# Latent attention keys in pairs of heads, with the shared rotated rows prepared once a layer

## What is computed

```python
def mla_mixer(c_q, c_kv, k_rope, ...):
    q = (rms_norm(c_q, q_norm_g) @ w_uq).reshape(b, t, MLA_HEADS, MLA_QK)
    kv = (rms_norm(c_kv, kv_norm_g) @ w_ukv).reshape(b, t, MLA_HEADS, MLA_NOPE + MLA_V)
    k_nope, v = kv[..., :MLA_NOPE], kv[..., MLA_NOPE:]
    k_r = jnp.broadcast_to(k_rope[:, :, None, :], (b, t, MLA_HEADS, MLA_ROPE))
    k = jnp.concatenate([k_r, k_nope], axis=-1)
    q = apply_partial_rope(rms_norm(q, q_head_g), cos, sin)
    k = apply_partial_rope(rms_norm(k, k_head_g), cos, sin)
    # softmax(q k^T / sqrt(96)) v per head, then an rms_norm over all heads
```

## Time and profile before

| | |
|---|---|
| time, median of 3 runs | 2167.85 us (2161.13 to 2168.57) |
| profiled execution: its time | 2165.82 us |
| profiled execution: span from first to last instruction | 2164.0 us |
| mean granted TensorE clock | 0.987 |

### The profile page before, as it was taken

How to read it: one execution, slowest core, us unless ns; L and a number is a source line. 1 busy time by engine, 2 the same in 40 slices (tenths; PEclk the granted TensorE clock), 3 DMA queues, 4 the chain that set the end, 5 groups by cost and what they waited for, 6 DMA issues and landing times.

```text
span 2164.0 us, 32558 instructions
## 1 busy us (share of the span) xinstructions
PE 2022.3 (93%) x13234; PEld 1754.1 (81%) x13234; DVE 1085.6 (50%) x1721; ACT 830.9 (38%) x1364; POOL 1001.9 (46%) x593
## 2 busy tenths in 40 slices
PE   7999998889789999999999999988888899999999
PEld 7988987567668999999999889885565577888887
DVE  7533377666765544441037332676656765444300
ACT  4322343677563222222234222444666623222211
POOL 4365444774323444444434455337853234444443
PEclk9999999999999999999999999999999999999999
DMA  4211112000002222223322111111000022323333
GB/s 167 70 59 60 60 49 69 10 1 30 21 20 60 89 95 90 88 89 98 98 87 79 59 59 59 51 58 40 1 20 30 20 81 94 95 91 97 98 102 112
DMA packets 40325, 143.80 MB, mean 66 GB/s; under 512 B 4592, under 2 KB 4976, under 8 KB 40048
## 3 DMA queue, kind: packets, MB, share of 16 engines
q1 hardware_dynamic: 40176, 141.72, 20.6%
HBM read 139.60 MB, written 2.10 MB: 65 GB/s over the span
## 4 chain that ended last, share of the span: by engine, by line
PE 75%; DVE 12%; ACT 7%; issue 5%; POOL 1%; DMA 0%; SPq 0%; DVEq 0%; ACTq 0%; POOLq 0%
PE pb L873 35%; PE pb L908 7%; PE pb L909 7%; PE pb L910 7%; PE pb L946 4%; PE pb L948 3%; PE pb L947 3%; DVE rowmax L2004 2%; PE pb L1331 2%; PE pb L1323 1%; ACT rstd L1480 1%; ACT ebuf L1515 1%; PE pb L1032 1%; ACT proj_r L1536 1%; POOL parts L651 1%
## 5 line engine op out<-in xcount | busy, mean ns | idle before, releaser
L651 POOL TENSOR_TENSOR parts<-raw,parts 128x1024 fp32r<-128x1024 f32 x248 | 606.8, 2447 | 791.8 <-ACT parts L1574 791.7
L1574 ACT ACTIVATE parts<-raw 128x1024 fp32r<-128x1024 f32 x248 | 262.5, 1059 | 834.5 <-PE pb L873 405.4
L873 PE MATMUL pb<-proj_r,parts 128*128 128x264 f32 x3104 | 427.5, 285 | 0.5 <-POOL parts L651 0.5
L873 PEld LDWEIGHTS pb<-proj_r,parts 128*128 128x128 f32 x3104 | 399.3, 189 | 0.8 <-issue 0.7
L873 PE MATMUL pb<-mix,parts 128*128 128x264 f32 x2208 | 333.7, 293 | 22.1 <-DVE mix L1906 13.1
L873 PEld LDWEIGHTS pb<-mix,parts 128*128 128x128 f32 x2208 | 299.3, 195 | 26.7 <-DVE mix L1906 13.5
L946 PE MATMUL pb<-mix,parts 128*128 128x264 f32 x800 | 242.9, 304 | 1.3 <-DVE proj L1939 1.3
L948 PE MATMUL pb<-mix,parts 128*128 128x264 f32 x800 | 229.8, 287 | 0.0
L947 PE MATMUL pb<-mix,parts 128*128 128x264 f32 x800 | 229.5, 287 | 0.0
L908 PE MATMUL pb<-proj_r,parts 128*128 128x512 f32 x528 | 207.5, 393 | 0.8 <-DVE mbuf L1930 0.8
L910 PE MATMUL pb<-proj_r,parts 128*128 128x512 f32 x528 | 207.7, 393 | 0.0
(11 more groups left out here) (290 smaller groups left out, 3288.8 us busy)
## 6 DMA issues: line engine op xcount, KB each, us to landing
raw<-w_stream SPq DMA_DIRECT2D x250, 512.0 KB, 3.5
w_head<-w_heads SPq DMA_DIRECT2D x8, 512.0 KB, 4.0
h<-x_t SPq DMA_DIRECT2D x8, 264.0 KB, 4.7
out_t<-h SPq DMA_DIRECT2D x8, 256.0 KB, 4.8
con<-consts SPq DMA_DIRECT2D x1, 1652.5 KB, 9.9
par<-params SPq DMA_DIRECT2D x1, 170.0 KB, 6.8
par<-params SPq DMA_DIRECT2D x1, 166.0 KB, 6.1
con<-consts SPq DMA_DIRECT2D x1, 128.0 KB, 6.6
```

The costliest lines, as they stand in the source:

```text
L651: nc.gpsimd.tensor_tensor(parts[:, n % PARTS, 1, :], w, parts[:, n % PARTS, 0, :].bitcast(FP32), ALU.subtract).then_inc(split.sem, 1)
L873: last = nc.tensor.matmul(pb[rows_, 2 * p + a, 0:HALF], lhs_t, rhs[:, a * HALF:(a + 1) * HALF], start=start, stop=stop)
L1574: nc.scalar.activation(parts[:, n % PARTS, 0, :], raw[:, r % RAW, :], ACT.Copy).then_inc(lead_ready.sem, 1)
```

## The change

Keys are prepared for two heads (2m and 2m+1) at a time: one product of 128 weight columns, one copy of 128 rows into a tile KK, one square, one sum with ones_h (a block matrix that sums rows 0 to 63 and 64 to 127 apart), one logarithm and exponential into a tile RSTD_K. VectorE then writes the 64 own rows of each of the two heads with its gain and factor. The shared rows are squared once a layer (rope_square, ScalarE, slot 57), turned and multiplied by the gain once a layer (rope_turn, GpSimd, slot 61), and summed once (rope_sum, first in the opening). For each pair GpSimd adds that sum to the squares (key_square) and scales the shared rows for both heads (key_rows), where it rotated before. PREPS has 12 entries instead of 16. The pair's stages 3 and 4 stand in the turns of heads 0, 2 and 4; the turns of heads 1, 3 and 5 prepare a query only. mixed_split comes in two blocks of four tiles. The key weights are loaded so that a pair's columns lie side by side, by four DMAs with runs of 64 numbers, where there was one DMA with runs of 4 KB; the gain of the upper 64 rows is loaded by two small DMAs at the start.

```diff
-PREPS = [(0, 0), (0, 1), (1, 0), (1, 1)] + [(hd, side) for hd in range(2, MLA_H) for side in (1, 0)]
+PREPS = [(0, 0), (0, 1), (1, 0)] + [e for m in range(1, MLA_H // 2) for e in ((m, 1), (2 * m, 0), (2 * m + 1, 0))]
+KK, RSTD_K, ROPE_SUM = MQ, MQ + 1, MK
...
+               + [(57, "rope_square", 0)] + [(61, "rope", 0)]
...
-        OPENING = (("p", 0, 0), ("p", 1, 0), ("t", 0, 0), ("p", 3, 0), ("t", 1, 0), ("p", 2, 0), ("v", 3, 0), ("t", 2, 0), ("p", 4, 0),
-                   ("p", 0, 1), ("p", 1, 1), ("t", 3, 0), ("t", 4, 0), ("v", 4, 0), ("p", 2, 1), ("p", 3, 1), ("v", 0, 0), ("v", 1, 0),
-                   ("p", 4, 1), ("v", 2, 0))
+        OPENING = (("r", 0, 0), ("p", 0, 0), ("p", 1, 0), ("t", 0, 0), ("p", 3, 0), ("t", 1, 0), ("p", 2, 0), ("v", 3, 0), ("t", 2, 0),
+                   ("p", 4, 0), ("p", 0, 1), ("p", 1, 1), ("t", 3, 0), ("t", 4, 0), ("v", 4, 0), ("p", 2, 1), ("v", 0, 0), ("v", 1, 0),
+                   ("v", 2, 0))
...
-                    prep(stage, hd + 2)
+                    if stage < 3:
+                        prep(stage, hd + 2)
+                    elif hd % 2 == 0:
+                        prep(stage, hd // 2 + 1)
...
+                        for a in range(2):
+                            for b in range(2):
+                                sp.dma_start(to[:, :, a, b, :], src[:, :, a, b, :]).then_inc(head_in[0].sem, 16)
...
+            def key_square(l, e):
+
+                s = SQ_M + e
+                pool.wait_ge(rope_summed.sem, rope_summed.at(l, 1))
+                pool.wait_ge(sq_ready.sem, sq_ready.at(l, s + 1))
+                nc.gpsimd.tensor_tensor(sq[:, s % 2, :], sq[:, s % 2, :], tile_of(proj, ROPE_SUM), ALU.add).then_inc(k_added.sem, 1)
+                pool.wait_ge(k_added.sem, k_added.at(l, PREPS[e][0] + 1))
+
+            def key_rows(l, e):
+
+                m, low, both = PREPS[e][0], slice(0, 48), slice(MLA_NOPE, MLA_ROWS)
+                pool.wait_ge(rs_ready.sem, rs_ready.at(l, RS_M + e + 1))
+                pool.wait_ge(rope_low.sem, rope_low.at(l, 1))
+                pool.wait_ge(s_ps.sem, s_ps.at(l, max(2 * m - 1, 0) * n_q(l)))
+                link(nc.gpsimd.tensor_tensor(k_head(2 * m)[both, :], tile_of(proj, MISC, rows_=low), tile_of(proj, RSTD_K, rows_=low), ALU.mult))
+                nc.gpsimd.tensor_tensor(k_head(2 * m + 1)[both, :], tile_of(proj, MISC, rows_=both), tile_of(proj, RSTD_K, rows_=both),
+                                        ALU.mult).then_inc(roped.sem, 1)
...
+                link(nc.gpsimd.memset(turned[64:96, :], 0.0))
+                link(nc.gpsimd.tensor_scalar(own[both, :], own[both, :], par_at(l, "kh_g", rows_=both), None, ALU.mult))
+                link(nc.gpsimd.tensor_tensor(turned[second, :], own[first, :], C("sin_m", first), ALU.mult))
+                link(nc.gpsimd.tensor_tensor(turned[first, :], own[second, :], C("sin_m", second), ALU.mult))
+                link(nc.gpsimd.tensor_tensor(own[both, :], own[both, :], C("cos_m", both), ALU.mult))
+                nc.gpsimd.tensor_tensor(own[both, :], own[both, :], turned[both, :], ALU.add).then_inc(rope_turned.sem, 1)
...
-                for e in range(2 * MLA_H):
+                for e, (n, side) in enumerate(PREPS):
+                    if side:
+                        key_square(l, e)
+                        key_rows(l, e)
+                        continue
...
-                    if e % 2 and 1 <= e // 2 <= KD // 2:
-                        mixed_split(l, e - 3)
-                        mixed_split(l, e - 2)
+                    if n in (2, 4):
+                        for k in range(2 * n - 4, 2 * n):
+                            mixed_split(l, k)
...
                     else:
                         pe.wait_ge(p_copy.sem, p_copy.at(l, e + 1))
-                        norm_sum(l, SQ_M + e, 1, p, rws)
+                        if side:
+                            pe.wait_ge(k_added.sem, k_added.at(l, n + 1))
+                        norm_sum(l, SQ_M + e, 1, p, rws, "ones_h" if side else "ones")
...
+                    elif stage == 4:
+                        dve.wait_ge(s_ps.sem, s_ps.at(l, max(2 * n - 1, 0) * n_q(l)))
+                        dve.wait_ge(rs_ready.sem, rs_ready.at(l, RS_M + e + 1))
+                        high = slice(MLA_NOPE, 2 * MLA_NOPE)
+                        for rows_, gain, dst in ((nope, par_at(l, "kh_g", rows_=nope), k_head(2 * n)),
+                                                 (high, gain_k[high, l, 0:1], k_head(2 * n + 1))):
+                            last = nc.vector.scalar_tensor_tensor(out=dst[nope, :], in0=tile_of(proj, KK, rows_=rows_), scalar=gain,
+                                                                  in1=tile_of(proj, RSTD_K, rows_=rows_), op0=ALU.mult, op1=ALU.mult)
```

More of the change, by code:

```diff
@@ L223, in trunk @@
         gain_d = sb("gain_d", [P, 1])
+        gain_k = sb("gain_k", [P, DEPTH, 2])
         eps = sb("eps", [P, 1])
@@ L424, in trunk, with prep_pair, opening @@
         OUT_BANK = (4, 5, 5, 4, 5)
-        def prep_pair(hd, side):
-            return ((0, 1), (3, 1))[hd][side] if hd < 2 else 3
-        def opening(value, turned_out, prep):
-            for what, k, hd in OPENING:
+        def prep_pair(n, side):
+            return side if n == 0 else 3
+        def opening(value, turned_out, prep, rope_sum):
+            for what, k, n in OPENING:
                 if what == "p":
-                    prep(k, hd)
+                    prep(k, n)
+                elif what == "r":
+                    rope_sum()
                 elif what == "t":
@@ L608, in _ @@
             sp.dma_start(par[:, 1:DEPTH, :], params[:, 1:DEPTH, :]).then_inc(par_in.sem, 16)
+            for l in range(DEPTH):
+                a = PARAM["kh_g"][0]
+                sp.dma_start(gain_k[MLA_NOPE:2 * MLA_NOPE, l, :], params[0:MLA_NOPE, l, a:a + 2]).then_inc(par_in.sem, 16)
             sp.dma_start(con[:, 0:2 * P], consts[:, 0:2 * P]).then_inc(const_in.sem, 16)
@@ L662, in rotate @@
             def rotate(l, e):
-                hd, side = PREPS[e]
-                buf, half = k_head(hd) if side else qh[:, hd % 2, 0:T], MLA_ROPE // 2
+                hd, half = PREPS[e][0], MLA_ROPE // 2
+                buf = qh[:, hd % 2, 0:T]
                 first, second, both = slice(64, 64 + half), slice(96, 96 + half), slice(MLA_NOPE, MLA_ROWS)
@@ new lines, in rope_turn @@
+            def rope_turn(l):
+                half = MLA_ROPE // 2
+                first, second, both = slice(64, 64 + half), slice(96, 96 + half), slice(MLA_NOPE, MLA_ROWS)
+                own, turned = tile_of(proj, MISC), qh[:, 0, 0:T]
+                pool.wait_ge(split.sem, split.at(l, G_SSD + 61 // PIECES + 2))
+                pool.wait_ge(o_ready.sem, o_ready.at(l, 1))
+                pool.wait_ge(rope_squared.sem, rope_squared.at(l, 1))
+                pool.wait_ge(c_ps.sem, c_ps.at(l, N_STATE))
+                link(nc.gpsimd.memset(turned[64:96, :], 0.0))
[4 more added lines that the diff above has]
+                nc.gpsimd.tensor_tensor(own[both, :], own[both, :], turned[both, :], ALU.add).then_inc(rope_turned.sem, 1)
+                pool.wait_ge(rope_turned.sem, rope_turned.at(l, 1))
@@ L809, in ml_job @@
                     cosines(l, n)
+                elif what == "rope":
+                    rope_turn(l)
             for l in range(DEPTH):
@@ L1353, in mlstm_turned @@
                     out_transposes(l, TR_OM + i, to_features(o_ml), i)
-                opening(v_product, mlstm_turned, prep)
+                opening(v_product, mlstm_turned, prep, rope_sum)
                 pe.wait_ge(v_ready.sem, v_ready.at(l, NT))
@@ L1764, in _, with prep @@
                 rws = slice(0, MLA_ROWS)
[L1766 removed]
+                def prep(stage, n):
                     side = stage // 3
[L1768 removed]
+                    e = PREPS.index((n, side))
                     if stage in (1, 3):
@@ L1771, in prep, with rope_sum @@
                         act.wait_ge(sq_used.sem, sq_used.at(l, SQ_M + e - 1))
-                        nc.scalar.activation(sq[rws, (SQ_M + e) % 2, :], k_head(hd)[rws, :] if side else qh[rws, hd % 2, 0:T],
-                                             ACT.Square).then_inc(sq_ready.sem, 1)
+                        if side:
+                            nc.scalar.activation(sq[:, (SQ_M + e) % 2, :], tile_of(proj, KK), ACT.Square).then_inc(sq_ready.sem, 1)
+                        else:
+                            nc.scalar.activation(sq[rws, (SQ_M + e) % 2, :], qh[rws, n % 2, 0:T], ACT.Square).then_inc(sq_ready.sem, 1)
                     elif stage in (2, 4):
                         act.wait_ge(rs_used.sem, rs_used.at(l, 11 + e))
-                        rsqrt(l, SQ_M + e + 1, prep_pair(hd, side), MLA_QK, rstd2, rws)
+                        if stage == 2:
+                            rsqrt(l, SQ_M + e + 1, prep_pair(n, side), MLA_QK, rstd2, rws)
+                        else:
+                            if n:
```

(9 more changed lines are left out.)

102 lines of the change are left out of this document (65 added, 37 removed).

## The result

The changed kernel takes 2193.32 us, median of 4 runs (2190.45 to 2194.91), the one before 2166.46 beside it: ratio 1.0127, 95% interval 1.0113 to 1.0141, so 26.9 us slower. The forecast was 2178 (+10.1), between 2162 and 2196: the sign and the range held, the size did not. The profiled execution took 2190.45 us, span 2188.6, against 2165.82 and 2164.0.

A forecast was written before the change was run, and what follows sets the result against it. No engine was taken as full: four pass work around, so prices were read as timeline gaps. 13.0 + 9.4 - 15.3 + 3.0 = +10.1 us on 2165.8 gave about 2178, range 2162 to 2196.

The forecast's parts named there:

- Step 1: Opening: the pair's sum waits for GpSimd's add queued behind query 0's rotation; +6.5 us per layer, +13.0 in all.
- Step 2: Heads 0, 2, 4: VectorE's two multiplications and GpSimd's shared-row ones disturb each other; +9.4 us over both layers.
- VectorE first: Even heads' pair: VectorE's first multiplication, then GpSimd's, then VectorE's second, in alternation; 2.6 us.
- Step 5: Edits at no cost, among them mixed_split in blocks of four and short key-weight DMA runs; 1 us if a block ran over.
- rival C: Key-weight loads: a 256-byte packet costs like a long one, so weights land late, 12.6 us per layer; 2203, 10%.
- Step 3: Heads 1, 3, 5, which prepare no key: shorter gaps between transposes; -15.3 us over both layers.
- Rival D: Odd heads gain nothing, since ScalarE's exponential, scaling and copy set the beat; 2193, 5%.
- Step 4: Slot 61: rope_turn on GpSimd delays VectorE's multiplications and the half evacuation behind them; 1.5 us per layer, +3.0.
- B: All removed TensorE work is on the path and the opening's wait is hidden: 22 us go, 2146; 7%.
- E: The two engines hardly disturb each other and the clock doesn't fall: -3.2 us, 2165; 14%.
- the forecast's own part of it: Whole kernel: the forecast's own case, 2165 to 2192 around 2178; 64%.

The follow-up runs named there:

- e1: Changed kernel with only GpSimd's opening order changed: the first key pair's add stands ahead of query 0's rotation; 2177.70 us, ratio 1.0053.
- e2: Changed kernel with one wait changed: GpSimd multiplies the shared rows after VectorE's two multiplications of the pair; 2180.12 us, ratio 1.0070.
- e3: Changed kernel with GpSimd's add ahead of query 0's rotation and its shared-row multiplication after VectorE's pair; 2165.36 us, ratio 1.000.
- e4: As e3, but TensorE adds the shared rows' squares by a 48-row product, with no add on GpSimd; 2164.66 us, ratio 0.999.
- e9: As e3, with the eight mixed_splits in four blocks of two, behind the rotations of queries 1, 2, 4 and 6; 2160.82 us, ratio 0.9983.
- e6: As e3, with GpSimd's turning of the shared rows moved from slot 61 to slot 90; 2162.28 us, ratio 0.9984.
- the filler: Changed kernel with six unused products on TensorE ahead of the wait for GpSimd's add in the opening; 2193.14 us, ratio 1.0131.

## Why the prediction was wrong, step by step

**Step 1, the opening: right in its mechanism, 3.4 us short.** Forecast +13.0, measured +16.4. The add was forecast to end at 379.8 and ended at 380.1; the gap was forecast at 7.4 and was 7.15; e1 shows that nothing else was in it. Short were VectorE's pair (3.6 instead of 2.6) and, in layer 1, the clock. There the value tile of 16 rows and the sum behind it ran at half clock too (2.43 and 2.13 us against 1.89 and 1.16 in layer 0).

**Step 2, the even heads: the step that failed.** Forecast +9.4, measured +26.7: 16.3 in layer 0, where the upper bound was 9, and 10.4 in layer 1, where it was 7.4. Those 17 us are nearly all of the miss; the other three steps together were 2.7 over, and the untouched stretches took some back. Four things were in it, shown on head 2 of layer 0, +6.6:
- The contention was taken in the middle (2.6) of its bounds and came out near the upper one (3.75): 3.64, and 3.61 to 3.66 in all eight pairs. e2 took the overlap away: 1.53. Together with the clock that brought the fourth gap of the head from 6.46 to 4.36. I had chosen "VectorE first"; the rows start VectorE 0.02 or 0.03 us ahead of GpSimd and GpSimd goes first all the same.
- I priced the clock only in the opening. In the loop, too, a late VectorE left TensorE 2.19 and 1.14 us idle, and the three groups behind lost 3.5 us by half clock (2.10, 1.97, 4.29 against 1.13, 1.05, 2.70), more than the contention did. In e3, where the first of the two waits is gone and the second still 1.14, they take 1.13, 1.05 and 2.70. The row for it stood in the earlier trace rows (a fall after 1.94 us), and the forecast used it in one place only.
- GpSimd's add, which was to be hidden behind the query's product, is not: TensorE waits 1.55 us for it, and the third gap is 4.11 where it was 3.46 (0.5 and 1.1 more in heads 0 and 4). e4 did without the add and has 3.61.
- The block of four mixed_split, below, 0.6.

**Step 5, the edits at no cost: one of them cost.** "If the block ran over, 1 us" looked at what stands behind the block on GpSimd, and not at what runs beside its end on VectorE. The earlier trace rows are exactly that meeting. e9 against e3 prices it, in the kernel with both edits: 2165.4 to 2160.8 by the medians, 5.0 in the loop of layer 0. In the kernel after it cost little: it shows in the first gap of head 2 (3.37 against 2.80), and head 4's is as before (2.80 against 2.79). The short DMA runs did cost nothing (table of loads, stretch 355 to 362): the four loads of 128 KB land 3.7 us after issue (median), like the one of 512 KB, and were issued by 360.6, so rival C is refuted.

```profile
w_head<-w_heads SPq DMA_DIRECT2D x4, 128.0 KB, 3.7
```

**Step 3, the odd heads: right.** Forecast -15.3, measured -17.4 (8.5 in layer 0, 8.9 in layer 1). In layer 0 the two gaps came to 2.24, forecast 2.4; that the first and last gap of the head would shrink too (2.68 to 2.30, 5.94 to 5.62) was not foreseen. In layer 1 the sum had a term without a row: 3.31 less 3.01 is 0.3, not 0.8; the gap went to 2.90, by 0.4, and the gap of 5.01 to 2.76 instead of 3.01, which made up for it. Rival D had the measured time, 2193, by the wrong mechanism: it needed these gaps not to shrink.

**Step 4, the turning: near in size, wrong in its place.** Forecast +3.0, measured +4.4. The four multiplications barely noticed (3.17 for 2.81); instead GpSimd waited for them (L728 took 2.13, and 1.61 in e6). The price came by way of the late split, which I had called harmless because TensorE has a tile's time. TensorE has; VectorE's two small operations that then ran beside the split and its follower have not (2.04 and 1.24 for 0.59 and 0.16). e6 confirms the 2.5 us by making them vanish.

**The rivals.** B (everything on the path) and E (little disturbance) fell with the traces. None of them was "the contention at its upper bound, with the clock falling in each even head", though both pieces were in the text: 3.75 as a bound, the fall as a row. That 2193 lies in the stated range is luck: the forecast's own part of it ended at 2192, and the rest up to 2196 was there for D. The bounds of the terms had been kept apart, when they share a cause: in head 2 the clock fell with VectorE's lateness and stayed at full speed without it (e3).

Open is why the untouched stretches differ by 5.4 us between the two profiles. 1.65 are a fall of the clock, and the 3.2 before layer 1's slots lie where the clock differs in part; why it differs there was not found.

## What to carry to other kernels

When work moves to an engine that another one waits for, write down that engine's queue order and ask of each new operation what stands behind it and what two-operand operation of VectorE runs beside it; GpSimd's add behind a rotation (7 us), splits ahead of an add (5 us) and splits beside a normalization (1 us and the clock) were all found that way, too late. Price TensorE's wait and the half clock behind it as one thing: the 2.1 us that the overlap put on VectorE's pair cost head 2 4.8 us (its last two gaps, 15.75 us in the kernel after and 10.92 in e3). And a change that removes TensorE work and adds waits can be mended by order: three edits of GpSimd's order took it from 1.3% slower to 0.2% faster than the kernel before, and a product of 48 rows in the place of GpSimd's add to 0.3%.

## What the runs showed of the hardware

VectorE's multiplication of 64 rows takes 0.76 us alone and 1.89 or 1.90 beside a GpSimd operation of 1.30 that the records start 0.02 or 0.03 us later, in all eight pairs of the kernel after. The Trainium skill has in "SBUF — State Buffer", section "Who interferes with whom", that the one that starts first has the shared ports and the other blocks. The trace agrees in the main that one stands for the length of the other's instruction: VectorE ends 0.57 after GpSimd, so no more than 0.2 of its 0.76 was done beside it. It doesn't agree on which, as far as starts 0.02 us apart can tell it. It goes the other way too: GpSimd's L728 took 2.13 us beside a chain of four VectorE multiplications that had begun 0.7 us before it, and 1.61 in e6, where they do not meet.

Being small did not help the blocked one: an operation on 4 columns took 2.04 us instead of 0.59 beside a split of 1024 columns. And the fall of the granted clock behind a wait was moved to a later wait by the filler, and not saved.
